# Seven normalisation roots by square root and reciprocal, eight moved multiplications and three moved copies

## What is computed

```
def _layer_norm(x, g, b):
    mu = jnp.mean(xf, axis=-1, keepdims=True)
    var = jnp.mean(jnp.square(xf - mu), axis=-1, keepdims=True)
    y = (xf - mu) * lax.rsqrt(var + LN_EPS)
    return (y * g.astype(F32) + b.astype(F32)).astype(x.dtype)

def rmsnorm(x, g):
    y = x32 * lax.rsqrt(jnp.mean(x32 * x32, axis=-1, keepdims=True) + EPS)
    return (y * g.astype(jnp.float32)).astype(x.dtype)
```

## Time and profile before

| | us |
|---|---|
| median of 3 runs | 2697.46 |
| lowest, highest | 2695.24, 2699.9 |
| the profiled execution's own time | 2695.71 |
| its span, first to last instruction | 2693.9 |
| TensorE busy in the span | 2622.9 |
| VectorE busy | 1671.8 |
| ScalarE busy | 1271.5 |
| mean granted TensorE clock | 0.997 of full speed |

### The profile page before, as it was taken

One profiled execution on the slowest core, in us unless ns is written; L12 is line 12 of the kernel. 1 busy time (PEld: TensorE's weight loads), 2 busy tenths in 40 slices (PEclk: granted clock), 3 DMA queues, 4 the chain that ended last, 5 costly groups with the idle time before them and its releaser, 6 DMA issues.

```text
span 2693.9 us, 42474 instructions
## 1 busy us (share of the span) xinstructions
PE 2622.9 (97%) x16495; PEld 2238.9 (83%) x16495; DVE 1671.8 (62%) x2896; ACT 1271.5 (47%) x2055; POOL 183.3 (7%) x234
## 2 busy tenths in 40 slices
PE   7999999999999999999999999989999999999998
PEld 6877789999998898779898776756877777799996
DVE  3445487265475465477265535865589986686784
ACT  3446455154364354356154444255365564475561
POOL 1110100000000000000000012051000000000000
PEclk9999999999999999999999999999999999999999
DMA  9985836957747565746547978922333333254451
GB/s 350 214 211 114 202 87 200 241 169 236 168 137 222 148 176 145 234 108 190 154 158 246 260 178 258 257 58 75 138 99 118 116 111 110 79 188 149 157 172 55
DMA packets 187721, 450.55 MB, mean 167 GB/s; under 512 B 14984, under 2 KB 31368, under 8 KB 186896
## 3 DMA queue, kind: packets, MB, share of 16 engines
q1 hardware_dynamic: 108368, 264.29, 28.9%
q0 software_dynamic: 60000, 167.78, 26.4%
q10 hardware_dynamic: 19168, 15.93, 2.0%
HBM read 438.24 MB, written 159.51 MB: 222 GB/s over the span
## 4 chain that ended last, share of the span: by engine, by line
PE 84%; DVE 8%; ACT 4%; issue 3%; DMA 1%; POOL 0%; ACTq 0%; DVEq 0%; POOLq 0%
PE ps L399 29%; PE ps L1514 24%; PE ps L549 6%; PE ps L3310 4%; PE ps L2322 2%; PE ps L1959 2%; PE ps L2113 2%; PE ps L1997 2%; PE ps L2858 2%; PE ps L786 2%; PE ps L914 1%; DVE w_lo L370 1%; ACT w_hi L362 1%; PE ps L873 1%; DVE xs L3011 1%
## 5 line engine op out<-in xcount | busy, mean ns | idle before, releaser
L370 DVE TENSOR_TENSOR w_lo<-raw,w_hi 128x1024 fp32r<-128x1024 f32 x500 | 611.1, 1222 | 473.4 <-ACT w_hi L362 472.4
L362 ACT ACTIVATE w_hi<-raw 128x1024 fp32r<-128x1024 f32 x500 | 527.0, 1055 | 514.4 <-PE ps L399 295.8
L1514 PE MATMUL ps<-x_hi,w_hi 128*128 128x264 f32 (+1 forms) x1120 | 317.4, 283 | 2.2 <-DVE rg L1893 0.7
L1514 PE MATMUL ps<-x_hi,w_lo 128*128 128x264 f32 (+1 forms) x1120 | 316.3, 282 | 0.0
L1514 PE MATMUL ps<-x_lo,w_hi 128*128 128x264 f32 (+1 forms) x1120 | 316.0, 282 | 0.0
L399 PE MATMUL ps<-x_hi,w_hi 128*128 128x512 f32 (+1 forms) x688 | 249.5, 380 | 24.4 <-DVE w_lo L370 17.5
L399 PE MATMUL ps<-x_lo,w_hi 128*128 128x512 f32 (+1 forms) x688 | 245.1, 374 | 0.0
L399 PE MATMUL ps<-x_hi,w_lo 128*128 128x512 f32 (+1 forms) x688 | 244.2, 372 | 0.0
L1514 PEld LDWEIGHTS ps<-x_hi,w_hi 128*128 128x128 f32 x1120 | 210.8, 188 | 5.1 <-issue 2.2
L1514 PEld LDWEIGHTS ps<-x_hi,w_lo 128*128 128x128 f32 x1120 | 211.1, 188 | 0.0
L1514 PEld LDWEIGHTS ps<-x_lo,w_hi 128*128 128x128 f32 x1120 | 210.6, 188 | 0.4
(11 more groups left out here) (500 smaller groups left out, 5833.2 us busy)
## 6 DMA issues: line engine op xcount, KB each, us to landing
raw<-in_weights SPq DMA_DIRECT2D x255, 512.0 KB
raw<-weight_sums SPq DMA_DIRECT2D x280, 256.0 KB
weight_sums<-in_weights POOLq DMA_DIRECT2D x36, 1536.0 KB, 19.6
raw<-in_weights SPq DMA_DIRECT2D x210, 256.0 KB
weight_sums<-in_weights POOLq DMA_DIRECT2D x12, 2048.0 KB, 31.5
weight_sums<-in_weights POOLq DMA_DIRECT2D x12, 1792.0 KB, 22.6
weight_sums<-weight_sums POOLq DMA_DIRECT2D x12, 1536.0 KB, 14.3
weight_sums<-weight_sums POOLq DMA_DIRECT2D x4, 2048.0 KB, 20.2
```

Of the source, the lines that this page charges most:

```text
L362: nc.scalar.activation(w_hi[:, s], raw[:, s], ACT.Copy).then_inc(hi_ready, 1)
L370: nc.vector.tensor_tensor(w_lo[:, s], raw[:, s], w_hi[:, s], ALU.subtract).then_inc(lo_ready, 1)
L1514: last = nc.tensor.matmul(out_, w[:, s, 4 * (b % 2) + k], a, start=kind in "125" and k == n == 0, stop=k == 3 and n == 2, skip_group_check ...
```

## The change

It has four parts.

1. Roots. In the seven norms, `load_root` and `square_root` replace `load_logarithm` and `inverse_root`: ScalarE computes only the square root of v + eps, and VectorE takes the reciprocal in place (`invert`) before its first product with it. The other users of `inverse_root` keep it.
2. `Norm`'s wait for the LayerNorm's y moves: ScalarE no longer waits for it where the squares were made ahead (`rms_mix`), and VectorE waits for it before `invert`.
3. `ln11` with `rms_mix`. ScalarE makes the squares of `rms_mix` straight from `xc` with scale g and bias b, and the first two tiles of y (`Y_ON_ACT` = 2). VectorE makes the other six, after its last product with the root.
4. `sparse_act`. `kept_act` moves from the end of a step to its start.

```diff
+        def load_root():
+            nc.scalar.activation(small[:, 14:15], small[:, 13:14], ACT.Sqrt)
+        def square_root(act, out, i, done, eps=RMS_EPS):
+            e = 12 if eps == LN_EPS else 13
+            nc.scalar.activation(out, i, ACT.Sqrt, bias=small[:, e:e + 1]).then_inc(done, 1)
+        def invert(dve, rt):
+            dve_chain.mark(nc.vector.reciprocal(rt, rt))
+            dve_chain.settle(dve)
...
             def dve(self, dve):
                 dve.wait_ge(norm_root, self.n + 1)
+                dve.wait_ge(norm_y, KT * self.nl)
+                invert(dve, self.rt[:, META:T])
...
                 tiles_out(act, self.tile)
-                wait(act, norm_y, KT * self.nl)
+                if not squared:
+                    wait(act, norm_y, KT * self.nl)
...
-                load_logarithm()
+                load_root()
                 act.wait_ge(norm_var, self.n + 1)
-                inverse_root(act, [(self.rt[:, META:T], flat[:, 3072:3072 + SEQ])], self.rt[:, META:T], norm_root)
+                square_root(act, self.rt[:, META:T], flat[:, 3072:3072 + SEQ], norm_root)
...
                 dve.wait_ge(norm_root, self.n + 1)
+                invert(dve, self.rt[:, c])
...
+                for k in range(self.Y_ON_ACT, KT) if self.last else ():
+                    dve.wait_ge(norm_scaled, KT * self.n + k + 1)
+                    nc.vector.tensor_scalar(x32[:, k, c], self.xc[:, k, c], par[:, self.g + k:self.g + k + 1],
+                                            par[:, self.b + k:self.b + k + 1], ALU.mult, ALU.add).then_inc(norm_y, 1)
...
                 for k in range(KT):
                     act.wait_ge(norm_scaled, KT * self.n + k + 1)
-                    y = x32[:, k, c]
-                    nc.scalar.activation(y, self.xc[:, k, c], ACT.Identity, scale=par[:, self.g + k:self.g + k + 1],
-                                         bias=par[:, self.b + k:self.b + k + 1]).then_inc(norm_y, 1)
-                    act.wait_ge(norm_y, KT * self.nl + k + 1)
+                    y, g, b = x32[:, k, c], par[:, self.g + k:self.g + k + 1], par[:, self.b + k:self.b + k + 1]
                     if follow:
-                        nc.scalar.activation(follow.sq[:, k, follow.c0:T], x32[:, k, follow.c0:T], ACT.Square).then_inc(norm_squared, 1)
+                        nc.scalar.activation(follow.sq[:, k, c], self.xc[:, k, c], ACT.Square, scale=g, bias=b).then_inc(norm_squared, 1)
+                    if not follow or k < self.Y_ON_ACT:
+                        nc.scalar.activation(y, self.xc[:, k, c], ACT.Identity, scale=g, bias=b).then_inc(norm_y, 1)
                     if not self.last:
+                        act.wait_ge(norm_y, KT * self.nl + k + 1)
                         nc.scalar.activation(x_hi[:, k, c], y, ACT.Copy).then_inc(norm_hi, 1)
...
         def sparse_act(act):
             for s in range(ND + VALUE_LAG):
+                for n in range(KEPT_EARLY, len(KEPT)):
+                    if fill_step[n, KT - 1] + 1 == s:
+                        kept_act(act, n)
                 if s < ND:
                     d_exp(act, s)
...
-                    if fill_step[n, KT - 1] + 1 == s:
-                        kept_act(act, n)
```

More of the change, by code:

```diff
@@ L1352, in summed_before @@
                 return (KT - 2) * self.nl
-            LESS_FIRST = 5
+            LESS_FIRST, Y_ON_ACT = 5, 2
             def dve(self, dve):
@@ L1392, in act @@
                 nc.scalar.activation(self.mean_sq[:, c], self.mean[:, c], ACT.Square).then_inc(ln_copied, 1)
-                load_logarithm()
+                load_root()
                 act.wait_ge(ln_centred, (KT + 1) * self.nl + 2)
-                inverse_root(act, [(self.rt[:, c], self.rt[:, c])], self.rt[:, c], norm_root, LN_EPS)
+                square_root(act, self.rt[:, c], self.rt[:, c], norm_root, LN_EPS)
                 for k in range(KT):
                     act.wait_ge(norm_scaled, KT * self.n + k + 1)
-                    y = x32[:, k, c]
-                    nc.scalar.activation(y, self.xc[:, k, c], ACT.Identity, scale=par[:, self.g + k:self.g + k + 1],
-                                         bias=par[:, self.b + k:self.b + k + 1]).then_inc(norm_y, 1)
-                    act.wait_ge(norm_y, KT * self.nl + k + 1)
+                    y, g, b = x32[:, k, c], par[:, self.g + k:self.g + k + 1], par[:, self.b + k:self.b + k + 1]
                     if follow:
-                        nc.scalar.activation(follow.sq[:, k, follow.c0:T], x32[:, k, follow.c0:T], ACT.Square).then_inc(norm_squared, 1)
+                        nc.scalar.activation(follow.sq[:, k, c], self.xc[:, k, c], ACT.Square, scale=g, bias=b).then_inc(norm_squared, 1)
+                    if not follow or k < self.Y_ON_ACT:
+                        nc.scalar.activation(y, self.xc[:, k, c], ACT.Identity, scale=g, bias=b).then_inc(norm_y, 1)
                     if not self.last:
+                        act.wait_ge(norm_y, KT * self.nl + k + 1)
                         nc.scalar.activation(x_hi[:, k, c], y, ACT.Copy).then_inc(norm_hi, 1)
```

## The result

| | before | after |
|---|---|---|
| median, us (7 runs each) | 2697.46 | 2704.73 |
| lowest, highest | 2694.88, 2699.90 | 2702.83, 2706.74 |
| profiled execution, its span | 2695.71, 2693.9 | 2704.16, 2702.4 |
| mean granted TensorE clock | 0.997 | 0.994 |

A forecast was written before the change was run, and what follows sets the result against it. Time is won or lost only where TensorE (97% busy) stands still or does products without a use. 10.7 - 1.5 + 3.0 - 4.9 + 6.4 = +13.7 us on the 2697.46 median gives 2711 us, range 2693 to 2724.

The forecast's parts named there:

- step 1: Four LayerNorms: VectorE's 3.4 us wait goes, but the wide reciprocals lie wholly on the path; +10.7 us.
- three readings: Wide reciprocal from the trace: usual rate 0.54 us, 13 ns over two columns 3.47 us, or all on the second 6.7 us.
- Step 2: From ln11 to rms_mix: earlier squares and sums, VectorE's six y covered by the square root; -1.5 us.
- Step 3: rms_ffn and final: 1.97 us of load and exponential go, 3.47 us of reciprocal comes, at each; +3.0 us.
- Step 4: Sparse attention: with kept_act moved, TensorE's two waits for the kept copy and the half clock go; -4.9 us.
- Step 5: Table loads: ten go, seven counted in steps 1 to 3, three beside the wait for the variance; nothing.
- Step 6: TensorE's clock: one fall to half speed at each of the four LayerNorms, 1.6 us each; +6.4 us.
- sum without falls: All terms but the clock's falls, for a reciprocal of R us: 7R - 17.1 us, zero at R = 2.4.
- copies without effect: Rival in the sparse attention: kept_act still waits, so the -4.9 us falls away, 2716 us; chance 0.05.
- cheap or middling reciprocal: Two rivals at the norms: reciprocal 0.6 us, 2686 us, chance 0.19; or 1.8 to 2.5 us, about 2695, chance 0.08.

The follow-up runs named there:

- y_only: The kernel before with only the edit after ln11 (eight squares from xc, six y on VectorE, the moved wait); 2694.63 us, 0.9992 of the kernel before.
- cover: The changed kernel with 13 more idle products of TensorE at each LayerNorm's root and 8 more at rms_mix and rms_ffn; 2699.83 us, 1.0010 of the kernel before.
- kept_only: The kernel before with only kept_act moved to the head of its step; 2690.06 us, 0.9976 of the kernel before.
- roots_only: The changed kernel with the kept_act and ln11 edits undone, square roots and wide reciprocals kept; 2717.46 us, 1.0073 of the kernel before.
- rms_roots: The changed kernel with logarithm and exponential back at the four LayerNorms; 2691.03 us, 0.9980 of the kernel before.
- widths: The changed kernel with each of the seven reciprocals cut in two pieces, the first of 16 to 384 columns; one run, 2704.81 us.
- one_root: The kernel before with kept_act moved, the edit after ln11, and one ScalarE Abs_reciprocal_sqrt at the seven norms, no VectorE reciprocal; 2678.78 us, 0.9932.

## Why the prediction was right, and where its sizes were off

It said slower, by 13.7 us, and it is slower by 7.3. The steps, in its own numbering:

- **The reciprocal and step 1 held.** 3.47 us was taken from 13 ns between a 2-column reciprocal and a copy, at 6.5 ns a column; the chip has 6.24 ns a column and 3.35 us. The division of the 13 ns over two columns was the right one of the three readings. That it came within 4% is partly luck: the 32 rows lie between 153 and 164 ns, and one ns there is a quarter of a microsecond for the wide tile. The Trainium skill's page "VectorE: DVE Perf Modes", section "Walkthrough: the 8-slice pipeline in each mode", read as eight cycles a column, gave an estimated 8.3 ns; the measurement is a quarter below that and decides. TensorE's resumption at `ln00` moved by 2.60 us (7.73 to 10.33 after its last sum), predicted 2.8.
- **Step 2 held in its mechanism, and gave more than its -1.5.** The squares came earlier, and the six y were hidden, as the idle time behind them shows. The sums did set the root's start, as predicted, but a pair of them was priced at 0.97 us, and at full clock twelve in a row take 5.42 us (`y_only`, `cover`), about 0.9 a pair. From the last sum of `ln11` to TensorE's resumption behind `rms_mix` `cover`, at full clock, takes 0.5 us longer than the kernel before, where the prediction without its fall says 1.1; the fall during the sums adds 1.2, not 1.6. So the piece came out 0.9 us below the predicted one.
- **Step 3 held.** +1.45 us to TensorE's resumption at `rms_ffn` (5.87 to 7.32 after its last sum) and +1.5 at `final`, both predicted as 1.5. No subtraction stands ahead of the root in these norms, so nothing covers it.
- **Step 4 was mis-sized**: -4.9 predicted, -6.5 by the time of `kept_only` and by the marks. At the first place the half clock had slowed not only line 2517's two matmuls but the four of line 2542 behind them (1.68 us, now 1.13): 3.9 in place of 3.1. At the second 2.0 in place of 1.75, and the copy in the tail, counted as nothing, gave 0.6 as the attention's output projection begins: a wait of 0.34 us before one of TensorE's `att_hi` matmuls is gone (line 399, at 1867.52 before). Why that one does so was not tested.
- **Step 5 was not tested by itself.** The ledger has no room for more than a few tenths in it.
- **Step 6 has the largest single error**: +6.4 predicted; `cover` gives 4.9 by the times and 4.5 by the marks, from five falls, not four. A fall was priced at what a fully busy TensorE loses (1.6 us), but behind a norm TensorE follows VectorE's `x_lo`, and part of the half speed only replaces waits: 0.5 to 1.2 us each in this execution. And one came where none was counted, at `rms_ffn`, with a wait of 2.25 us.

Which of the two short waits brings a fall is not settled by their length. In the traces of the changed kernel, `roots_only`, `rms_roots` and `widths` TensorE waits 2.06 or 2.07 us at `rms_mix` and 2.24 to 2.26 us at `rms_ffn`. In the changed kernel the clock held at the first and fell at the second; in `roots_only` it was the other way round, in `rms_roots` it fell at both, and in `widths` at neither. The stretches behind `rms_mix` and `rms_ffn` in `roots_only`, behind `rms_mix` in `rms_roots`, and behind `rms_ffn` in `widths`:

```profile
1574.00:1578.00 4.00, 4.00 (x12) 3.17 (x11) 4.00 (x7) 2.10 (x4) 0.00 (x0) 0.57 0.00 0
2350.00:2354.00 4.00, 3.40 (x15) 2.82 (x16) 4.00 (x7) 2.10 (x4) 0.00 (x0) 1.00 0.00 0
1564.00:1568.00 4.00, 4.00 (x12) 3.09 (x12) 4.00 (x8) 2.11 (x4) 0.00 (x0) 0.57 0.00 0
2337.00:2341.00 4.00, 3.39 (x15) 2.83 (x16) 4.00 (x7) 2.10 (x4) 0.00 (x0) 1.00 0.00 0
```

So the number of falls in one execution is in part chance. The prediction counted none at these two places and kept 2 x 1.6 us for the range, which was right: such a fall moved TensorE by 1.6 us at `rms_mix` in `roots_only` and cost 1.1 us at `rms_ffn` here.

Between +13.7 and +8.5 of the ledger lie 5.2 us: 1.9 in step 6, 1.7 in step 4, some 0.9 in steps 1 and 2 together and 0.8 from the start of the kernel, all of one sign (5.3 by these rounded terms). None of them could have turned the verdict, since the reciprocal is well above the 2.4 us at which the prediction's sum without falls changes its sign. The rival "copies without effect" is refuted by `kept_only`, and the cheap or middling reciprocal by its rows.

## What to carry to other kernels

Before an operation is moved to another engine, look for it in the trace at any size: two widths, or one and a copy, give a price per column, and it can be five or six times the usual (3.35 us here, against 0.54 to 0.74 for other operations on 512 columns). What counts is not which engine is less busy, but whether the operation has cover there: the 1.97 us of table load and exponential lay 1.1 us deep behind VectorE's own subtractions, while the 3.35 us of reciprocal in VectorE's own queue had none. And where an engine must stand still for longer, fill the time with work without use before judging the change: about two thirds of this net loss was the clock. But count a fall of the clock only for the time in which the engine would not have waited anyway.

## What the runs showed of the chip that I had not expected

- A VectorE reciprocal costs 145 ns + 6.24 ns a column of float32 (16 to 528 columns, `widths` and the changed kernel), some 50 ns less directly behind another one; the other single-tile operations of these traces take 0.54 to 0.74 us for 512 columns, 1.1 to 1.4 ns a column with all included.
- ScalarE's `Abs_reciprocal_sqrt` over 128x512 takes 0.67 to 0.72 us, the same as its logarithm and its square root.
- The clock's falls are not tied to the change alone. In the profiled execution of `rms_roots` it stood at half level for 12 us in the first block, in a stage that is the same in all kernels here, and in that of `one_root` for 11 us (234 to 245, mean 0.53); in the changed kernel's execution it held there. The rows of both, `rms_roots` first (length, busy times, granted clock, DMA share, GB/s):

```profile
234.00:246.00 12.00, 12.00 (x36) 7.51 (x35) 1.51 (x8) 6.54 (x15) 1.88 (x2) 0.50 0.22 37
```

```profile
234.00:246.00 12.00, 12.00 (x66) 8.16 (x66) 4.56 (x13) 7.71 (x22) 1.88 (x2) 1.00 0.40 80
```

That execution's span was 2697.8 us, against a median of 2691.03 for the kernel: so one kernel's runs differ by several us for no reason in its program (2688.3 to 2699.6 over 12 runs here), and a difference of 2 us needs the marks in the traces, not the times. What decides on such a fall stays open.
